# Slot transposes behind the scatter, and gathered rows split in the turn that gathers them

## What is computed

```python
def swiglu(h, w_gate, w_up, w_down):
    return (jax.nn.silu(h @ w_gate) * (h @ w_up)) @ w_down
...
def expert_block(args):
    tok, wt, e = args
    xb = h_pad[tok]
    y = (jax.nn.silu(xb @ w_gate[e]) * (xb @ w_up[e])) @ w_down[e]
    return y * wt[:, None].astype(h.dtype)
```

## Time and profile before

| | us |
|---|---|
| median of 3 runs | 1835.73 |
| lowest, highest | 1835.28, 1836.89 |
| span of the profiled execution | 1835.7 |
| TensorE busy (matmuls), share of the span | 1770.4, 96% |
| VectorE busy | 1389.9, 76% |
| ScalarE busy | 1189.7, 65% |
| the expert loop, roughly | 812 to 1822 |

### The profile page before, as it was taken

The page is one execution under the profiler, slowest core; times in us unless marked ns, Lnnn a source line. Parts: engine busy times, 40 slices in busy tenths (PEclk is TensorE's granted clock), DMA queues, the critical chain, the costliest instruction groups (busy, mean ns, idle before and its releaser), DMA issues.

```text
span 1835.7 us, 28966 instructions
## 1 busy us (share of the span) xinstructions
PE 1770.4 (96%) x9816; PEld 1519.2 (83%) x9816; DVE 1389.9 (76%) x1506; ACT 1189.7 (65%) x1419; POOL 23.1 (1%) x49
## 2 busy tenths in 40 slices
PE   7999999999998999979999999999999999999997
PEld 6888897899987889868888888888888888888886
DVE  5666574454546664769989989899899899898996
ACT  5465553344434655457877778777777777777775
POOL 2000000000000000000000000000000000000000
PEclk9999998999998999979999999999999999999999
DMA  8544344566655443669989989999999899899990
GB/s 290 164 133 116 119 151 148 166 187 180 187 161 148 127 121 109 227 239 340 373 318 369 370 311 373 347 331 373 338 348 371 314 371 369 305 375 351 332 372 27
DMA packets 213291, 475.01 MB, mean 259 GB/s; under 512 B 14704, under 2 KB 16768, under 8 KB 213232
## 3 DMA queue, kind: packets, MB, share of 16 engines
q1 hardware_dynamic: 212016, 470.61, 74.1%
q0 software_dynamic: 1216, 3.61, 0.6%
HBM read 473.11 MB, written 1.05 MB: 258 GB/s over the span
## 4 chain that ended last, share of the span: by engine, by line
PE 88%; ACT 4%; DVE 4%; issue 3%; DMA 0%; POOL 0%; ACTq 0%; DVEq 0%; POOLq 0%
PE ps L1631 79%; PE ps L1974 2%; PE ps L2007 1%; PE ps L1840 1%; ACT probs L1000 1%; PE ps L1823 1%; ACT whi L865 1%; PE ps L1810 1%; DVE wlo L1169 1%; DVE gates L1187 1%; PE ps L1812 0%; ACT probs L992 0%; PE ps L1894 0%; DMA gain<-in_g_mem 0%; PE ps L1682 0%
## 5 line engine op out<-in xcount | busy, mean ns | idle before, releaser
L1169 DVE TENSOR_TENSOR wlo<-raw,whi 128x1024 fp32r<-128x1024 f32 (+1 forms) x766 | 915.2, 1219 | 326.6 <-ACT whi L865 295.1
L865 ACT ACTIVATE whi<-raw 128x1024 fp32r<-128x1024 f32 (+1 forms) x766 | 796.9, 1055 | 336.3 <-PE ps L1631 333.7
L1631 PE MATMUL ps<-whi,xg_hi 128*128 128x512 f32 x896 | 357.9, 399 | 2.4 <-DVE xg_lo L1175 2.4
L1631 PE MATMUL ps<-wlo,xg_hi 128*128 128x512 f32 x896 | 352.1, 393 | 0.0
L1631 PE MATMUL ps<-whi,xg_lo 128*128 128x512 f32 x896 | 349.9, 391 | 0.0
L1631 PE MATMUL ps<-hT_hi,whi 128*128 128x256 f32 x960 | 277.7, 289 | 6.3 <-ACT gates L875 2.9
L1631 PE MATMUL ps<-hT_lo,whi 128*128 128x256 f32 x960 | 273.4, 285 | 0.0
L1631 PE MATMUL ps<-hT_hi,wlo 128*128 128x256 f32 x960 | 273.0, 284 | 0.0
L1631 PEld LDWEIGHTS ps<-whi,xg_hi 128*128 128x128 f32 x896 | 169.1, 189 | 38.3 <-DVE wlo L1169 5.3
L1631 PEld LDWEIGHTS ps<-wlo,xg_hi 128*128 128x128 f32 x896 | 168.8, 188 | 38.6
L1631 PEld LDWEIGHTS ps<-whi,xg_lo 128*128 128x128 f32 x896 | 169.0, 189 | 35.3
(11 more groups left out here) (299 smaller groups left out, 2120.6 us busy)
## 6 DMA issues: line engine op xcount, KB each, us to landing
raw<-in_w_down_exp SPq DMA_DIRECT2D x200, 512.0 KB, 5.1
raw<-in_w_gate_exp SPq DMA_DIRECT2D x184, 512.0 KB, 5.1
raw<-in_w_up_exp SPq DMA_DIRECT2D x160, 512.0 KB, 5.4
raw<-in_w_in SPq DMA_DIRECT2D x72, 512.0 KB, 3.7
kM<-in_w_up_exp SPq DMA_DIRECT2D x40, 512.0 KB, 5.7
raw<-in_w_gate_dense SPq DMA_DIRECT2D x28, 512.0 KB, 4.2
raw<-in_w_up_dense SPq DMA_DIRECT2D x28, 512.0 KB, 4.1
raw<-in_w_down_dense SPq DMA_DIRECT2D x28, 512.0 KB, 4.3
```

What stands on the lines that cost most here:

```text
L865: s.activation(whi[n % SPLIT][:, 0:w], raw[tile(key)][:, 0:w], ACT.Copy).then_inc(chunk_hi, 1)
L1169: v.tensor_tensor(wlo[n % SPLIT][:, 0:w], raw[tile(key)][:, 0:w], whi[n % SPLIT][:, 0:w].bitcast(F32), ALU.subtract).then_inc(chunk_split, 1)
L1631: ins = mm(o, lhsT, rhs, start=start and i == 0, stop=stop and i == 2, skip_group_check=True)
```

## The change

Two things move. The slot transposes go from behind group 1's gate and up chunks to the place between `scatter` and `transposed_act(0)`; they then use `onehot_next` and `cur_next`, which at that point still hold this turn's expert, write into the second half of `ps[1]`, and have a semaphore of their own (`back_full`). `cur` and `onehot` fall away. And the split of the gathered rows goes from the start of the next turn to the end of the turn that gathers them; for the first expert it goes ahead of the loop. On VectorE `actm_lo` of group 0 comes ahead of the additions into x, and the copies of `slot_w` and `back` right behind these.

```diff
@@ build_tally
             for half in range(2):
                 tl.add("psum_full3", ("gathered", "first", half))
+            for half in range(2):
+                areas["gather", half] = 3
+                tl.add("hi_copied", ("gathered", "first", half))
+                tl.add("psum_free3", ("gathered", "first", half))
             experts_from[0] = tl.count["chunk"]
             tl.enter_loop()
 
-            for half in range(2):
-                areas["gather", half] = 3
-                tl.add("hi_copied", ("gather", half))
-                tl.add("psum_free3", ("gather", half))
-            tl.add("routed", "onehot")
             tl.add("routed", "onehot_next")
...
-                    if g == 1:
-                        psum(("T_back",), 1)
                 elif g + 1 < GROUPS:
                     split(("moe", "T", g + 1), 1)
             for half in range(2):
                 tl.add("psum_full3", ("gathered", "next", half))
+                tl.add("hi_copied", ("gathered", "next", half))
+                tl.add("psum_free3", ("gathered", "next", half))
             tl.leave_loop(EXPERTS)
@@ ScalarE
             turns = s.value_load(turns_i[0:1, 0:1], min_val=EXPERTS, max_val=2 * EXPERTS)
+            def gathered_hi(turn):
+                for half in range(2):
+                    eng.wait_ge(psum_full[3], gathered_by(turn, half))
+                    s.activation(xg_hi[:, 4 * half:4 * (half + 1), :].rearrange("p k n -> p (k n)"),
+                                 ps[3][:, 512 * half:512 * (half + 1)], ACT.Copy).then_inc(hi_copied, 1)
+
+            gathered_hi(0)
             with s.Fori(0, turns) as e:
...
-                upto(2)
-
-                for half in range(2):
-                    eng.wait_ge(psum_full[3], gathered_by(e, half))
-                    s.activation(xg_hi[:, 4 * half:4 * (half + 1), :].rearrange("p k n -> p (k n)"),
-                                 ps[3][:, 512 * half:512 * (half + 1)], ACT.Copy).then_inc(hi_copied, 1)
                 upto(4)
...
                 upto(FFN_CHUNKS)
+                gathered_hi(e + 1)
@@ VectorE
+            def gathered_lo(turn):
+                for half in range(2):
+                    part = slice(4 * half, 4 * (half + 1))
+                    eng.wait_ge(hi_copied, gathered_by(turn, half, "hi_copied"))
+                    v.tensor_tensor(xg_lo[:, part, :].rearrange("p k n -> p (k n)"), ps[3][:, 512 * half:512 * (half + 1)],
+                                    xg_hi[:, part, :].rearrange("p k n -> p (k n)").bitcast(F32),
+                                    ALU.subtract).then_inc(psum_free[3], 1)
...
+            gathered_lo(0)
             with v.Fori(0, turns) as e:
...
-                upto(2)
-                for half in range(2):
-                    part = slice(4 * half, 4 * (half + 1))
-                    rest(("gather", half), xg_lo[:, part, :].rearrange("p k n -> p (k n)"),
-                         ps[3][:, 512 * half:512 * (half + 1)], xg_hi[:, part, :].rearrange("p k n -> p (k n)"), e)
                 upto(4)
...
                 upto(before_split(0))
+                moe_rest(0)
                 add_scattered(e)
-                moe_rest(0)
-                upto(before_split(0) + 2)
-
-                slots_of(e, cur, e * 2 + 1, onehot)
+                eng.wait_ge(back_full, e + 1)
+                v.tensor_copy(slot_w[:, :], ps[1][:, FF_GROUP + TOK:FF_GROUP + TOK + 1])
+                v.tensor_copy(back[:, :], ps[1][:, FF_GROUP:FF_GROUP + TOK])
                 upto(before_split(0) + 4)
-                slots_of(e + 1, cur_next, e * 2 + 2, onehot_next)
+                slots_of(e + 1)
                 for g in range(1, GROUPS):
                     upto(before_silu(g))
                     moe_product(g)
-                    if g == 1:
-                        wait_full(eng, ("T_back",), e)
-                        v.tensor_copy(slot_w[:, :], ps[1][:, TOK:TOK + 1])
-                        v.tensor_copy(back[:, :], ps[1][:, 0:TOK]).then_inc(psum_free[1], 1)
                     upto(before_split(g))
                     moe_rest(g)
                 upto(FFN_CHUNKS)
+                gathered_lo(e + 1)
@@ TensorE
                         if g == 0:
                             scatter(e)
+                            slots = onehot_next[:, :, :].bitcast(F32)
+                            for t in range(NT):
+                                mm(ps[1][:, FF_GROUP + TOK:FF_GROUP + TOK + 1], slots[:, t, :], cur_next[:, 2 + t:3 + t],
+                                   start=t == 0, stop=t == NT - 1)
+                            for t in range(NT):
+                                ins = nc.tensor.transpose(ps[1][:, FF_GROUP + P * t:FF_GROUP + P * (t + 1)], slots[:, t, :],
+                                                          ident[:, :])
+                            ins.then_inc(back_full, 1)
                             transposed_act(0)
-                        if g == 1:
-
-                            pe.wait_ge(routed_sem, tl.after("routed", "onehot", e))
-                            wait_free_in_loop(pe, ("T_back",), e)
-                            for t in range(NT):
-                                mm(ps[1][:, TOK:TOK + 1], onehot[:, t, :], cur[:, 2 + t:3 + t], start=t == 0, stop=t == NT - 1)
-                            for t in range(NT):
-                                ins = nc.tensor.transpose(ps[1][:, P * t:P * (t + 1)], onehot[:, t, :], ident[:, :])
-                            ins.then_inc(psum_full[1], 1)
```

21 lines of the change are left out of this document (10 added, 11 removed).

## The result

| | median | lowest to highest | runs | ratio to before, 95% interval |
|---|---|---|---|---|
| before | 1836.31 us | 1835.28 to 1837.47 | 4 | |
| after | 1848.73 us | 1847.19 to 1849.25 | 4 | 1.0066 [1.0054, 1.0078] |

The account below looks back on a forecast made before the run. The prediction took TensorE's own queue, plus its short waits for act_m and xg_lo, to bound each turn of the expert loop. Its sum was 1835.7 - 5.0 - 4.2 + 4.6 = 1831.1 us, range 1829.0 to 1834.4.

Parts of the forecast that it names:

- the steady pace: TensorE's matmuls in the expert loop: 23 steps from 1338.43 to 1343.70, read as 0.229 us per 128x512 matmul.
- Slot transposes: Moved between scatter and activation transposes, their 0.63 us per turn fits into 0.81 us free: 5.0 us gained over 8 turns.
- Rival E: Transposes moved but not covered, since act_m is late by as much: 1836.1 us, no change; chance 0.03.
- Turn boundary: Splitting gathered rows at the turn's end removes TensorE's xg_lo wait, 0.60 us at seven boundaries: 4.2 us gained.
- VectorE's queue behind act_m: Chunk 12's remainder still arrives just in time, 0.07 us of slack left: 0 lost, at most 1.6 us.
- Rival A: VectorE is late for chunk 12 every turn, 0.15 to 0.3 us per turn: 1832.3 to 1833.5 us; chance 0.20.
- Loop entry: Copies of gathered rows now stand ahead of the loop, so TensorE idles before the first gate matmul: 4.6 us lost once.
- Rival D: Loop entry costs nothing, because ScalarE's copies turn out not to hold back chunk 0: 1826.5 us; chance 0.04.
- rival B: Loop entry costs over 4.6 us: later clock rise (up to 1834.4) or dearer table load (1832.5 with drain); chance 0.13.
- The stretch at 1.2 GHz: After the first gate matmul the clock was assumed to stay at 1.2 GHz for the same 4.8 us, after the later start.
- End of the loop: The last turn's needless split of rows is hidden beside 24 down matmuls: 0; uncovered some 1.3 us, once.
- Rival C: Weights' transfers pace the turns, so both gains vanish and the entry's loss remains: 1840.3 us, slower; chance 0.05.

Follow-up runs that it names:

- a1: Changed kernel with an unused 32-byte tile in cur's old place, so xg and actm start at a multiple of 64 again: 1831.44 us, ratio 0.9972.
- a2: Kernel before with an unused 32-byte tile put in ahead of cur, order of instructions untouched: 1853.23 us, ratio 1.0093.
- b1: Kernel before with only the split of the gathered rows moved to the turn that gathers them: 1836.47 us, ratio 0.9997.
- b2: a1 with the split of the gathered rows back where it was, so only the slot transposes are moved: 1833.38 us, ratio 0.998.
- b3: a1 with one 128x1 silu ahead of the loop, so the silu table is loaded before it: 1831.82 us, ratio 0.9974.
- d1: a1 with 64 bytes more room ahead of xg_hi, putting xg and actm at offset 128 modulo 256: 1824.05 us, ratio 0.9933.
- d4: c1 with b3's silu ahead of the loop and four 32-byte rooms ahead of xg_hi (xg and actm at 128): 1812.9 us, ratio 0.9871.
- e2: Changed kernel with six small attention tiles merged, the silu ahead of the loop, six rooms ahead of xg_hi; hT and actT at 128: 1814.49 us, ratio 0.9879.
- e1: a1 with weights whi and wlo moved to offset 160 and xg and actm to 96 modulo 256: 1819.97 us, ratio 0.991.
- c1: Changed kernel with row_max and neg_max merged into one tile, moving hT, xg, actm and others by 32 bytes: 1837.15 us, ratio 1.0004.

## Why the prediction was wrong

**The step that failed** is the first paragraph's reading of the earlier trace rows: "the steady pace: 23 steps from 1338.43 to 1343.70, 0.229 us for a 128x512 matmul". I took 0.229 us for a constant of the instruction and carried it over to the changed kernel without saying so. It is a property of where two tiles lie. It came to 0.2333, 17.3 us over 4032 products, against a net forecast of 4.6 us. a1 and a2 show this: 32 bytes given back, and the changed kernel is at 1831.44; 32 bytes put in, and the kernel before is at 1853.23. None of the five rivals held it. The two lines of the diff that delete the tiles were read only as work that VectorE no longer does. A hint stood in the trace of before: the dense stage ran the same 128x512 instruction at 234.2 ns, at the same clock, and nothing in my argument could have said why.

The terms of the sum, one by one, as a1 and the halves b1 and b2 show them with the placement of before:

- **Slot transposes, 5.0 us.** Right. b2's turn is 0.59 us shorter, forecast 0.63 (8 turns: 4.7 us). The place is as forecast. From the last scatter matmul to the activation transposes 1.00 us pass in the changed kernel (1083.32 to 1084.32), where 1.04 did, and now the transposes are in it. The 0.2 us of standing still that I had expected are there too, though no row carries them as idle time, since the slot transposes' modelled end reaches up to the next row. act_m is done at 1083.50 + 0.69 = 1084.19 (VectorE's timeline, below), 0.13 before the transposes start, which is the reaction of the earlier trace rows; it is the same 0.13 in all eight turns of before, after and a1. So act_m still ends the wait, and b3 confirms it: where act_m comes early, the transposes start 0.84 after the scatter, and the slot instructions take 0.61 (1081.10 to 1081.71) where the sum had 0.63. Rival E is out.
- **Turn boundary, 4.2 us.** Right: 0.62 per turn, forecast 0.60. TensorE in the changed kernel goes from the last down to the first gate matmul in one step of 0.24:

```profile
1070.26 0.40 PE L1603 MATMUL ps<-wlo,actm_hi 128*128 128x512 f32 x1
1070.50 0.39 PE L1603 MATMUL ps<-whi,xg_hi 128*128 128x512 f32 x1
```

- **VectorE's queue behind act_m, 0.** Right. The order came as forecast: act_m, chunk 11's remainder, actm_lo, the additions into x, slot_w and back, then the remainders in one row of four without an idle time ahead:

```profile
1083.50 0.69 DVE L1559 TENSOR_TENSOR act_m<-ps,silu_m 128x512 f32<-128x512 f32 x1 [0.68 <-ACT silu_m L1090]
1084.45 1.23 DVE L1140 TENSOR_TENSOR wlo<-raw,whi 128x1024 fp32r<-128x1024 f32 x1 [0.25 <-ACT whi L834]
1085.64 0.69 DVE L1146 TENSOR_TENSOR actm_lo<-ps,actm_hi 128x512 fp32r<-128x512 f32 x1
1086.25 2.34 DVE L1543 TENSOR_TENSOR x<-ps,x 128x1024 f32<-128x1024 f32 x2
1088.51 0.15 DVE L1574 COPY slot_w<-ps 128x1 f32<-128x1 f32 x1
1088.58 0.41 DVE L1575 CAST back<-ps 128x256 fp32r<-128x256 f32 x1
1088.91 4.62 DVE L1140 TENSOR_TENSOR wlo<-raw,whi 128x1024 fp32r<-128x1024 f32 x4
```

  In a1, where TensorE runs at the step of before and asks for its chunks sooner, the waits of the seven turns name none of TensorE's own either. Rival A is out at this pace, but it was as close as the 0.07 us of slack said. In d1, which steps by 227.2 ns, the weight load for chunk 12, four chunks into group 1, waits for wlo in each of seven turns:

```profile
1084.83 0.19 PEld L1606 LDWEIGHTS ps<-whi,xg_hi 128*128 128x128 f32 x1 [0.17 <-DVE wlo L1143]
```

  The matmul behind it still starts 0.23 us after the one before (1084.70 to 1084.93), so it costs nothing there.
- **Loop entry, 4.6 us.** Right at 4.5. TensorE's entry in the changed kernel:

```profile
810.01 0.41 PE L1946 MATMUL ps<-onehot_next,normed_lo 128*128 128x128 f32 x1
814.74 0.80 PE L1603 MATMUL ps<-whi,xg_hi 128*128 128x512 f32 x1 [4.32 <-DVE wlo L1140]
...
818.75 0.40 PE L1603 MATMUL ps<-whi,xg_hi 128*128 128x512 f32 x1
```

  4.73 us from the last gather matmul, 0.22 before (812.03 to 812.25): 4.51 more, ended by wlo as forecast. The table load lies behind the second xg_hi with 0.01 us between, and the copy of chunk 0 follows it 0.02 us later. The Trainium skill's drain of about 1380 ns ("ScalarE: Activation LUTs", "What ACT_TABLE_LOAD costs") doesn't show here either, and b3 agrees: with the load of 1.28 us gone the entry is 1.42 us shorter, not 2.7. Rival D is out, and so is rival B: neither a dearer table load nor a later rise of the clock (next point) shows.
- **The stretch at 1.2 GHz, the same 4.8 us.** A little too long. Steps of 0.43 last from 814.74 to 818.75, 4.0 us, where 4.8 were before, so some 0.4 us came back. It also explains why a1's first turn is 1.59 us shorter than before and the others only 1.2.
- **End of the loop, 0.** Nothing shows that would contradict it, and it wasn't tested by itself.
- **Rival C, turns paced by transfers.** Out. From 1100 to 1150 us a1 moves 378 GB/s at a share of 1.02, the kernel before 375 at the same share, and d4's turns of 123.7 us are supplied as well.

So no term of the sum was off by more than 0.4 us, and its time was that of a1, not of the kernel that it was made for. The low chance of 0.05 for a slower kernel was a chance for C alone, a mechanism in the schedule. No case was left for a change of what a single instruction costs, though the diff changes the memory plan.

Open is why the distance matters at all, and why 0 and 64 are the good ones for 128x512 products and 64 alone for 128x256 ones. All distances seen are multiples of 32 bytes, all tiles fp32r, and no run here shows another type or a distance between. The period of 256 bytes is shown only in part: distances 0 and 128 differ, so it isn't 128, and modulo 512 the fast distance 0 stands for 256 (the expert loop of d1) and for 0 (the dense stage of e2) at the same step; the distance 64 was seen as 320 alone. Nor is the distance the only rule that fits: the exclusive or of the two offsets sorts every row of the table, and the 128x256 products, just as well, and no run parts the two.

## What to carry to other kernels

And a half that works (here 0.6 us per turn, twice) can hide behind a term that isn't in the sum, so a change is best judged by its parts in the trace and not by its total.

## What the runs showed of the hardware

- The pace of a 128x512 fp32r matmul at the full clock depends on the places of moving and stationary tile in SBUF together. By their distance modulo 256 bytes it is 227 ns at 0 (d1, d4, e2), 229 at 64 (before, a1, e1), 233 to 234 at 32, 96, 128, 160, 192 and 224.
- For 128x256 products (moving hT, stationary weights) it is 117.5 ns at 64 (c1, d4) and 119.8 to 119.9 at 0 and 96 (e2, before): the good distances aren't the same for both shapes.
- The profile counts TensorE as busy in either case. Its busy time in 50 us of a turn is 50.00 us before, after and in a1; only the distance of starts tells.
- A turn of the loop has two table loads of 1.28 us, at its head and ahead of its first silu, in all eight turns; one silu ahead of the loop removes both from all of them (b3). The second one had delayed act_m: without it the activation transposes start 0.2 us sooner.
